# Reciprocal square roots of the norms: eight dependent small VectorE operations instead of eleven

## The reference, cut to what matters

```python
def rms_norm(x, gain):                      # EPS = 1e-6
    x32 = x.astype(jnp.float32)
    y = x32 * lax.rsqrt(jnp.mean(x32 * x32, axis=-1, keepdims=True) + EPS)
    return (y * gain.astype(jnp.float32)).astype(x.dtype)
```

## Time and profile before

| | before |
|---|---|
| median of three runs | 1695.56 us |
| the profiled execution's own time | 1689.58 us |
| its span, first to last instruction | 1687.8 us |
| mean granted clock of PE, share of full | 0.959 |
| PE busy | 1552.3 us (92%) |
| DVE busy | 821.4 us (49%), 1470 instructions |
| ACT busy | 739.6 us (44%) |
| POOL busy | 596.5 us (35%) |

### The profile page before, as it was taken

The page is one execution under the profiler, slowest core; times in us unless marked ns, Lnnn a source line. Parts: engine busy times, 40 slices in busy tenths (PEclk is TensorE's granted clock), DMA queues, the critical chain, the costliest instruction groups (busy, mean ns, idle before and its releaser), DMA issues.

```text
span 1687.8 us, 23289 instructions
## 1 busy us (share of the span) xinstructions
PE 1552.3 (92%) x9590; PEld 1255.9 (74%) x9590; DVE 821.4 (49%) x1470; ACT 739.6 (44%) x1057; POOL 596.5 (35%) x227
## 2 busy tenths in 40 slices
PE   4999989998998999989889889999998898899997
PEld 4867867874997778568667658999886676489996
DVE  2734477323767764153664452522437833635222
ACT  3334366422436654143445344444434454444442
POOL 1200034320000442225555234655546442246543
PEclk7999889999998899999899999999999899999999
DMA  9597269669625686753343344555443333445550
GB/s 386 193 329 270 98 266 344 253 251 373 237 100 200 238 326 234 272 198 122 116 131 124 118 159 165 181 196 171 179 145 118 116 112 126 158 148 205 185 189 26
DMA packets 51225, 327.22 MB, mean 194 GB/s; under 512 B 5936, under 2 KB 5936, under 8 KB 17456
## 3 DMA queue, kind: packets, MB, share of 16 engines
q1 hardware_dynamic: 51120, 325.73, 53.3%
HBM read 324.66 MB, written 1.05 MB: 193 GB/s over the span
## 4 chain that ended last, share of the span: by engine, by line
PE 74%; DVE 17%; ACT 3%; DMA 3%; issue 1%; POOL 1%; DVEq 0%; SPq 0%; ACTq 0%
PE ps L224 19%; PE ps L226 18%; PE ps L225 18%; PE ps L221 14%; DVE lo L232 4%; DMA raw<-in_wmod 2%; DVE pb L2752 1%; ACT hi L229 1%; PE ps L2701 1%; DVE s L240 1%; DVE z L232 1%; ACT pb L229 1%; DMA raw<-in_wo_v 1%; DVE s L232 1%; DVE pb L232 1%
## 5 line engine op out<-in xcount | busy, mean ns | idle before, releaser
L232 POOL TENSOR_TENSOR lo<-raw,hi 128x2048 fp32r<-128x2048 f32 (+2 forms) x76 | 355.1, 4683 | 646.8 <-ACT hi L229 646.8
L229 ACT ACTIVATE hi<-raw 128x2048 fp32r<-128x2048 f32 (+2 forms) x192 | 350.7, 1858 | 55.8 <-POOL big L232 16.9
L232 DVE TENSOR_TENSOR lo<-raw,hi 128x2048 fp32r<-128x2048 f32 (+1 forms) x116 | 291.7, 2532 | 101.1 <-ACT hi L229 100.9
L232 POOL TENSOR_TENSOR loh<-rawh,hih 128x1024 fp32r<-128x1024 f32 x64 | 156.3, 2456 | 137.2 <-ACT hih L229 136.9
L224 PE MATMUL ps<-hTh,hi 128*128 128x256 f32 x640 | 183.2, 286 | 5.4 <-DVE hTl L232 2.9
L225 PE MATMUL ps<-hTl,hi 128*128 128x256 f32 x640 | 182.2, 285 | 0.0
L226 PE MATMUL ps<-hTh,lo 128*128 128x256 f32 x640 | 182.1, 285 | 0.0
L224 PE MATMUL ps<-hi,hTh 128*128 128x512 f32 (+3 forms) x320 | 119.6, 374 | 16.1 <-DVE lo L232 7.5
L224 PEld LDWEIGHTS ps<-hTh,hi 128*128 128x128 f32 x640 | 124.0, 194 | 7.2 <-issue 3.5
L225 PEld LDWEIGHTS ps<-hTl,hi 128*128 128x128 f32 x640 | 124.1, 194 | 0.5
L226 PEld LDWEIGHTS ps<-hTh,lo 128*128 128x128 f32 x640 | 123.9, 194 | 0.0
(11 more groups left out here) (306 smaller groups left out, 2986.6 us busy)
## 6 DMA issues: line engine op xcount, KB each, us to landing
raw<-in_wgu SPq DMA_DIRECT2D x64, 1024.0 KB, 5.0
raw<-in_wmod SPq DMA_DIRECT2D x48, 1024.0 KB, 6.9
raw<-in_wdn SPq DMA_DIRECT2D x32, 1024.0 KB, 5.7
rawh<-in_wgt SPq DMA_DIRECT2D x64, 512.0 KB, 3.8
raw<-in_wup SPq DMA_DIRECT2D x32, 1024.0 KB, 4.8
raw<-in_wdown SPq DMA_DIRECT2D x32, 1024.0 KB, 5.1
raw<-in_wz SPq DMA_DIRECT2D x12, 1024.0 KB, 4.7
raw<-in_wbr SPq DMA_DIRECT2D x8, 1024.0 KB, 4.8
```

What stands on the lines that cost most here:

```text
L229: return self.e.activation(o, a, f, **kw)
L232: return self.e.tensor_tensor(o, a, b, op)
```

## The change

The same function is computed with fewer dependent steps. Four edits:

- The sums of squares come out as means: ScalarE's `Square` gets `scale=1.0 / 32`, so that each square is divided by 1024 (in `a_stats` and `a_moe`).
- The addition of the two halves in `v_stats` becomes a `scalar_tensor_tensor` that adds EPS too, and the separate scaling operation of `v_rstd` is left out there (`inv_n` is None). The five other callers keep it.
- The shift and the subtraction on the bits become one `tensor_scalar` that multiplies by -0.5.
- The two iteration steps (seven operations) become the evaluation of one polynomial of the fourth degree in the product of the mean and the guess squared (six operations). Where `v_rstd` wrote its intermediate values to `tmp` alone, it now writes to `ss` too.

```diff
@@ -642,29 +642,27 @@
+    ROOT = 0.7235405817547222, -3.722988595072433, 5.6564527047170285, -4.5444396531968065, 2.4630066686385943
+
     def v_rstd(self, v, dst, ss, inv_n, tmp):
-        v.wait_ge(*v.last)
-        v.ts(ss, ss, inv_n, EPS, ALU.mult, ALU.add).then_inc(*v.up("dve"))
-        v.wait_ge(*v.last)
-        v.ts(tmp.bitcast(I32), ss.bitcast(I32), 1, None, ALU.arith_shift_right).then_inc(*v.up("dve"))
-        v.wait_ge(*v.last)
-        v.ts(dst.bitcast(I32), tmp.bitcast(I32), -1.0, 1597463007.0, ALU.mult, ALU.add).then_inc(*v.up("dve"))
-        v.wait_ge(*v.last)
-        v.stt(tmp, dst, -0.5, dst, ALU.mult, ALU.mult).then_inc(*v.up("dve"))
+        scale, *c = self.ROOT
+        v.wait_ge(*v.last)
+        if inv_n is not None:
+            v.ts(ss, ss, inv_n, EPS, ALU.mult, ALU.add).then_inc(*v.up("dve"))
+            v.wait_ge(*v.last)
+        v.ts(dst.bitcast(I32), ss.bitcast(I32), -0.5, 1597463007.0, ALU.mult, ALU.add).then_inc(*v.up("dve"))
+        v.wait_ge(*v.last)
+        v.stt(tmp, dst, scale, dst, ALU.mult, ALU.mult).then_inc(*v.up("dve"))
         v.wait_ge(*v.last)
         v.tt(tmp, tmp, ss, ALU.mult).then_inc(*v.up("dve"))
         v.wait_ge(*v.last)
-        v.stt(dst, tmp, 1.5, dst, ALU.add, ALU.mult).then_inc(*v.up("dve"))
-        c = 0.375 ** 0.5
-        v.wait_ge(*v.last)
-        v.tt(tmp, dst, dst, ALU.mult).then_inc(*v.up("dve"))
-        v.wait_ge(*v.last)
-        v.stt(tmp, tmp, c, ss, ALU.mult, ALU.mult).then_inc(*v.up("dve"))
-        v.wait_ge(*v.last)
-        v.stt(tmp, tmp, -1.25 / c, tmp, ALU.add, ALU.mult).then_inc(*v.up("dve"))
-        v.wait_ge(*v.last)
-        v.stt(dst, tmp, 1.875, dst, ALU.add, ALU.mult).then_inc(*v.up("dve"))
+        v.stt(ss, tmp, c[0], tmp, ALU.add, ALU.mult).then_inc(*v.up("dve"))
+        for x in c[1:3]:
+            v.wait_ge(*v.last)
+            v.stt(ss, ss, x, tmp, ALU.add, ALU.mult).then_inc(*v.up("dve"))
+        v.wait_ge(*v.last)
+        v.stt(dst, ss, c[3], dst, ALU.add, ALU.mult).then_inc(*v.up("dve"))
@@ -674,7 +672,7 @@  a_stats (the same in a_moe)
-                a.ac(buf[:, 0:512], src[:, t, 512 * h:512 * h + 512], ACT.Square,
+                a.ac(buf[:, 0:512], src[:, t, 512 * h:512 * h + 512], ACT.Square, scale=1.0 / 32,
@@ -682,8 +680,8 @@  v_stats
-        v.tt(ss, ss, self.st[:, c0 + 2:c0 + 4], ALU.add).then_inc(*v.up("dve"))
-        self.v_rstd(v, self.st[:, c0 + 4:c0 + 6], ss, 1.0 / 1024, self.st[:, c0 + 6:c0 + 8])
+        v.stt(ss, ss, EPS, self.st[:, c0 + 2:c0 + 4], ALU.add, ALU.add).then_inc(*v.up("dve"))
+        self.v_rstd(v, self.st[:, c0 + 4:c0 + 6], ss, None, self.st[:, c0 + 6:c0 + 8])
```

More of the change, by code:

```diff
@@ L1801, in a_moe @@
                     a.wait_ge(*a.last)
-                a.ac(self.s1[:, 0:512], self.x[:, t, 512 * h:512 * h + 512], ACT.Square,
+                a.ac(self.s1[:, 0:512], self.x[:, t, 512 * h:512 * h + 512], ACT.Square, scale=1.0 / 32,
                      accum_out=self.st[:, 2 * h + t:2 * h + t + 1]).then_inc(*a.up("act"))
```

## The result

| | before | after |
|---|---|---|
| median of seven runs each, same comparison | 1695.36 us (1693.17 to 1696.67) | 1688.04 us (1681.43 to 1689.51) |
| the profiled execution's own time | 1689.58 us | 1684.60 us |
| its span | 1687.8 us | 1682.8 us |
| mean granted clock of PE | 0.959 | 0.967 |
| DVE instructions | 1470 | 1430 |

The account below looks back on a forecast made before the run. PE holds 74% of the chain of waits, VectorE 17%; shortened VectorE groups count only there. Five places sum 0.59 + 0.41 + 0.41 + 0.41 + 0.59 = 2.41 us, taking 1695.56 to 1693.2 us, range 1690.8 to 1695.8.

Parts of the forecast that it names:

- b0: Norm b0, on the path into PE's products: three operations fewer, -0.59 us.
- gating: Gating path of the second mixer: two operations fewer, -0.41 us, coming through whole, just.
- latent rows: Latent rows of the two four-branch mixers: two operations fewer each, -0.41 us each, the uncertain part.
- end: Norm e, ahead of ScalarE's last scaling and the store: three operations fewer, -0.59 us, the surest term.
- the gating wait: PE's wait of 0.56 us near 452: still there after the change, with 0.15 us left.
- No gain was hidden: Rival: gating path and latent rows hidden by something else, only b0 and end count: 1.2 us, 1694.4; chance 0.15.
- no long operation came or went at the latent rows: Three long operations stay per latent group; rival of one 2.3 us wait less: 1690.9 us, chance 0.15 including a clock stretch.
- `scalar_tensor_tensor` did not slip past GpSimd: Rival at the latent rows: it passes GpSimd without waiting, z starts earlier: 3.2 us gain, 1692.4; chance 0.03.
- slower than before: Rival: one long wait of 2.3 us more in each mixer, +2.2 us in all, 1697.8; chance 0.07.
- a stretch of clock: Rival: 5 us at 1.2 GHz behind PE's wait for z costs 1.7 us; chance 0.15 together with one long wait less.
- sign of being wrong: A time change not made up by b0, gating path, both latent groups and end, above all a changed long-operation count.
- How the numbers follow: Part giving forecast chance 0.60, range 1690.8 to 1695.8 us, and 0.77 for a time within 0.2% of before.

Follow-up runs that it names:

- forty added operations: Kernel before with eight more operations at each of the five places counted on the path: 1700.51 us, ratio 1.0055, pooled +9.6 +/- 1.3 us.
- eighty off the path: Kernel before with eight more operations at each of the ten places counted as covered: 1690.25 us, ratio 0.9995, pooled -1.5 +/- 1.1 us against a counted +1.8.
- before again: Kernel before, unchanged, run again on chip A beside the same kernel: 1693.64 us against 1690.70, ratio 1.0013.
- after's third set: The changed kernel, unchanged, run again beside the kernel before on chip C: median of 12 runs 1687.75 us, ratio 0.9977.
- padded kernel: Changed kernel with its first product repeated three times (twice in the five other calls), restoring the old operation count: 1692.46 us, ratio 0.9996 to before.
- run 6: Not a label: words from "a profiled run 6 us off their median", meaning the profiled execution of the unchanged kernel before, 1689.58 us.

## Why the prediction was wrong

**The mechanism was right.** Price, places and cover came out as written: 0.2 us per operation; b0 0.60, gating 0.47 by ScalarE's instructions (0.43 at PE), latent rows 0.39 and 0.41, end 0.6; the gating wait down to what can't be listed; three long operations per latent group, the third of them a `scalar_tensor_tensor` in the first mixer, which the earlier trace rows did not show and for which the earlier trace rows were taken. No gain was hidden, no long operation came or went at the latent rows, `scalar_tensor_tensor` did not slip past GpSimd, and after was slower than before in none of the four comparisons. The rival that came nearest is "a stretch of clock": PE's mean clock did not stay at 0.96 but was 0.967 in the profiled run of after and 0.964 over its first seven. Small things were misread: PE's wait in the second mixer was 4.00 us and not 3.49, a long operation is eleven to twelve times the price of 0.2 and not fourteen, and the low parts behind c, of which the prediction says nothing, changed places. None of these enters the sum.

The prediction's own sign of being wrong came true in one part: a change of the time that the five groups do not make up.

**The step that failed is where the sum becomes a time: the starting point of 1695.56 us, and the width that "How the numbers follow" gives it; and then the size of the gain, 2.41 us passed on one to one.** The prediction starts from 1695.56, the median of three runs that lie within 1.3 us, and takes that as how well the kernel's time is known. It is not. The 107 later runs of before, on three chips, reach from 1685.70 to 1699.66 with a mean of 1692.0 and a scatter of 3.0 us; the medians of their four sets are 1690.70, 1692.76, 1693.22 and 1693.64. The first set (seven runs, all above 1693.1, median 1695.36) lies above these medians, by more than single runs' scatter explains: seven runs drawn from the 107 have so high a mean about three times in a thousand. The miss of 5.2 us (1693.2 against 1688.04) takes apart as:

- 3.6 us from the starting point: 1695.56 against 1692.0 for all the later runs. After has no such outlier: its four medians are 1688.04, 1687.19, 1687.75 and 1688.72.
- 1.6 +/- 0.6 us from the size of the gain, 4.0 against 2.4 (1.2 +/- 0.5 at equal clock).
- Nothing is left over. That it comes out so even is luck, as 1688.04 is one median of seven and 1692.0 a mean over three chips.

One number in the table of before said so: the profiled execution took 1689.58, 6.0 us less than the median of the three. The prediction noted that difference, added it back and drew no conclusion, where a single run that far out means a range of several us to either side. The bound of 0.2% for what a measurement can tell was about right; but by that width of scatter the chance of "faster by over 0.2%" could not be held at 0.20 with a count of 0.14%.

**What stays open.** Whether the 1.2 to 1.6 us above the count are real. They are 2.4 to 2.7 standard errors. With the first comparison in the fit, by times and with a level of its own, after is at -4.6 +/- 0.6 us, 3.7 errors beyond the count. The forty added operations give 0.24 +/- 0.03 us each, so 2.9 us for the twelve, between the count and the measured gain. And the eighty off the path missed their count by three errors with no cause found, so an excess of that size may be no more than what sets of runs differ by. What would make the excess is seen once: behind PE's lengthened wait at the gating path 1.5 us of low clock, in the kernel with forty operations more. The reverse, a shortened wait that spares such a stretch in after, can't be shown from the traces: of the stretches at 747 and 805 that after lacks, the first is missing in before again too (which has one 8 to 10 us earlier, as after has), and the second is 2.7 us long in before and 1.4 in before again, and after's third set has 1.4 us there. Nor is it settled why the first set of before was 3 us high, and whether the chip or the time it ran at did it; the low-clock total of its profiled run, 62.4 us, is that of the padded kernel, whose time was ordinary.

## What to carry to other kernels

Count the dependent operations where the next engine waits, and price them at the spacing of starts in the chain; fifteen places shrank to five and the sum held to tenths of a us in the trace. Then ask how well the time of the starting point is known: three runs that agree are no scatter, and a profiled run 6 us off their median is a warning that the same program lands several us apart from set to set. A change of 0.15% is read from matched instructions of two traces, which show it, and not from the difference of two medians, which may show three times as much.

## What the runs showed of the hardware

- PE's clock after the same wait is not the same from run to run. Behind 1.96 us of waiting in before and in after, one went on at 0.66 of full and one at 1.00, with 19 and 36 products in the same 5 us. Counted from the spacing of wide products, the total at the lower level was 47.6 to 62.4 us in the executions counted, and span and mean clock go together: 5.8 us per 0.01.
- At the latent rows one operation of GpSimd makes just one of VectorE's long, and all three kinds there can be the one: `tensor_scalar`, `tensor_tensor` and `scalar_tensor_tensor` on 128x4 all took about 2.3 us, until GpSimd's had ended. The Trainium skill (SBUF — State Buffer, Who interferes with whom) says that a VectorE instruction with two inputs from SBUF contends with a GpSimd one that reads SBUF. The trace agrees: four `scalar_tensor_tensor` took 2.80 us at 867.45 and 0.75 at b0. The `tensor_scalar`, which read one tile, were held as well (two took 4.66 us at 862.36). Moving GpSimd's work moves the long one to whatever VectorE does beside it.
- Between two large low parts that start together, a head start of under 0.1 us decided which engine's is long: 2.29 us for VectorE and 5.85 for GpSimd when VectorE was 0.07 us ahead, 5.85 and 3.78 when GpSimd was 0.08 ahead. Three small operations fewer turned it round, the same way in all executions profiled.
- A longer wait of PE may cost more than its length: grown from 0.56 to 2.22 us at the gating path, it was followed by 3.4 us at the lower level, 1.5 us of time, where there had been none. That was seen at one place, in one execution; as the clock differs behind equal waits too, it isn't shown that the wait made it.
